# Opening of a fused decoder layer: five weight blocks per strip in place of three, two of them through saved partial sums

## The chip, the cores and the metric

The kernel runs on one NeuronCore of a Trainium2 chip. The metric is the device time of one execution in microseconds. Of the kernel before there are three timed executions, with a median of 1898.13 us, and one more that was profiled.

## The reference, cut to what matters

One decoder layer on 256 tokens of width 2048, all in f32: a SwiGLU feed-forward, a token mixer, a second SwiGLU, each between norms that are modulated by nine vectors computed from `c`.

```python
D_MODEL, SEQ, D_FF, N_MOD = 2048, 256, 5504, 9

def swiglu(h, w_in, w_out):
    gate, up = jnp.split(h @ w_in, 2, axis=-1)
    return (jax.nn.silu(gate) * up) @ w_out

def sandwich(x, fn, g_pre, g_post, shift, scale, gate, res_w):
    h = rms_norm(x, g_pre) * (1.0 + scale[:, None]) + shift[:, None]
    y = rms_norm(fn(h), g_post)
    return x + res_w * gate[:, None] * y

def reference(...):
    cond = jax.nn.silu(c)
    mod = cond @ ada_w[l] + ada_b[l]                 # ada_w: 2048 x 18432
    sh1, sc1, gt1, sh2, sc2, gt2, sh3, sc3, gt3 = jnp.split(mod, N_MOD, axis=-1)
    x = sandwich(x, swiglu with ffn1_w_in, ffn1_w_out, norm_g[0], norm_g[1], sh1, sc1, gt1, 0.5)
    x = sandwich(x, token_mixer ...,                   norm_g[2], norm_g[3], sh2, sc2, gt2, 1.0)
    x = sandwich(x, swiglu with ffn2_w_in, ffn2_w_out, norm_g[4], norm_g[5], sh3, sc3, gt3, 0.5)
    return x
```

The change touches the start: the two vectors `sh1` and `sc1`, the modulated `h` of the first feed-forward, and the first column blocks of `h @ ffn1_w_in`.

## The kernel before

**Products in two parts.** Every weight is split on the chip into a rounded part and a rest: ScalarE copies `w_raw` to `w_hi` (L781 in the opening, L601 later), VectorE subtracts to get `w_lo` (L1286, L983). `xT` is split the same way. TensorE then makes three products for each chunk of 128 rows: hi by hi, lo by hi, hi by lo (L1557 to L1559, or L1790, L1791, L1796 where the parts of `xT` come late). A **unit** is two chunks for both tiles of 128 tokens, so 12 matmuls of 512 columns. A **block** is 512 columns of the feed-forward's input matrix over all 16 chunks: 8 units. Its result fills one of the four PSUM pairs `ps_g`, `ps_u`, `ps_t`, `ps_y` (two banks each, 128 x 512 for each tile of tokens). Eight units make a group; the first feed-forward has 33 groups (264 units), each with 4 loads of 1 MB on SyncE's queue. The ring of `w_hi` and `w_lo` has 4 places: ScalarE may write the one of unit v when unit v-4 has been used (`pe_used`), and `w_raw` has four slots of two units.

**The modulation vectors.** `cond @ ada_w` is no matmul here. VectorE multiplies each piece of `ada_w` by its 128 values of `cond` and adds it to an accumulator (L1270, L1273; later L1015, L1017 on whole rows of 2048), and TensorE sums over the partitions at the end. Vectors 0 and 1 (`sh1`, `sc1`) are needed before the first product. They are made in **strips** of columns, `STRIP_CHUNKS = ((0, 4), (4, 4), (8, 4), (12, 2), (14, 2))`: the columns of a strip are the rows of `xT` that the units of this strip need. A tile is 1 MB of `ada_w` (two loads, one for each vector), a strip of 4 chunks has 8 tiles, one of 2 chunks has 4. The tiles go round in four slots, and SyncE issues a tile when the one four before it has been used.

**The opening.** For each strip TensorE does the units of this strip for three blocks (`OPENING = 3`: the gate block 0 in `ps_g`, the up block 0 in `ps_u`, the gate block 1 in `ps_t`). All three stay in PSUM until the last strip, and `ps_y` serves the column sums. A strip of 4 chunks has 6 units, one of 2 chunks has 3. Ahead of the last unit of a strip TensorE runs filler matmuls (`warm`, L1655: 24, 24, 0, 0 calls), then `first_sums` of the next strip (L1780, L1781: 16 calls of one column, 8 for a short strip), then the last unit. VectorE makes the new columns of `modcol` (L1294 to L1296), ScalarE scales `xT_raw` and rounds it (L695, L698), VectorE makes the rest (L1302), and the next strip's units may start. The order of all this is written out by hand for each engine, as is the order of loads on SyncE's queue.

**After the opening.** Block 0 has both halves, so `h = silu(gate) * up` (L796, `h_mul` L1039), a transpose of `h` on TensorE (`transpose_h`, L1621, 8 calls) into `ps_t`, and its products with the output matrix (`out_group`). The groups then follow as in-gate, in-up, out for each block (`hidden`). Blocks that `on_vector` names are transposed by VectorE (`turn_hidden`, L1062) instead. From unit 24 on the six other modulation vectors of this layer's first half are made beside it: 96 tiles (`ada_raw`, 1 MB each, issued by GpSimd, L541), tile a after unit `24 + 12 * a // 5`. The accumulators of four of them are transposed and summed at blocks `ROWS_AT` (`turned_half` on TensorE, `column_sums` on VectorE, L1073).

## Time and profile before

| what | value |
|---|---|
| median of the three timed executions | 1898.13 us (1897.89 to 1899.44) |
| profiled execution, its own time | 1899.21 us |
| its span | 1897.4 us |
| TensorE busy in the span | 1854.0 us, 98% |
| VectorE busy | 1495.9 us, 79% |
| ScalarE busy | 856.9 us, 45% |
| moved by DMA | 486.84 MB, mean 257 GB/s |

The profiled time is 1.81 us above its span, and 1.08 us above the median. Busy time of TensorE counts every matmul, the filler calls too. In the page's picture of 40 slices (47.4 us each), TensorE is at nine tenths or more in all but the first, and the DMA engines are at nine tenths or more in the first fourteen and fall to five to seven tenths after that.

### The profile page before, as it was taken

What the parts mean: (1) busy time and instruction counts of PE and PEld (TensorE: products, weight loads), DVE (VectorE), ACT (ScalarE), POOL (GpSimd) and SP (SyncE); (2) the same over time, 40 slices, a digit from 0 to 9 for tenths busy, and PEclk for the clock granted to TensorE, in tenths of its full rate; (3) what the DMA queues carried; (4) which work ended last, traced back from release to release, by engine and by line L of the source; (5) the groups of instructions that cost most, each with busy time, mean ns of one, the idle gap of its engine ahead of it and who ended that gap; (6) DMA issues with size and microseconds to landing.
All of it is one profiled execution on the core that took longest, in us unless ns stands there. A gap on an engine that the chain in (4) does not pass through costs nothing.

```text
span 1897.4 us, 21957 instructions
## 1 busy us (share of the span) xinstructions
PE 1854.0 (98%) x8743; PEld 1545.2 (81%) x8743; DVE 1495.9 (79%) x1633; ACT 856.9 (45%) x1095; POOL 82.0 (4%) x151
## 2 busy tenths in 40 slices
PE   6999999999999999999999999999999999999997
PEld 6878888888888889877778887888888888888895
DVE  5989989999989989975876587677777785676576
ACT  4244443443443444574666446544444434443443
POOL 0001000000000000010000010000000000000000
PEclk9999999999999999999999999999999999999998
DMA  9999999999998999655444454666776655556552
GB/s 369 369 372 360 341 363 332 353 342 346 356 347 316 389 342 343 246 161 181 149 134 134 162 176 167 231 233 237 250 249 234 240 191 198 189 198 213 175 199 78
DMA packets 208677, 486.84 MB, mean 257 GB/s; under 512 B 8560, under 2 KB 29760, under 8 KB 193472
## 3 DMA queue, kind: packets, MB, share of 16 engines
q1 hardware_dynamic: 191648, 365.72, 55.9%
q0 software_dynamic: 16224, 117.47, 16.5%
q10 hardware_dynamic: 704, 2.25, 0.3%
q8 instruction: 69, 1.13, 0.2%
q14 instruction: 32, 0.26, 0.0%
HBM read 483.31 MB, written 2.10 MB: 256 GB/s over the span
## 4 chain that ended last, share of the span: by engine, by line
PE 83%; DVE 10%; DMA 2%; issue 2%; ACT 1%; SPq 1%; ACTq 0%; DVEq 0%; POOL 0%
PE ps_u L1557 10%; PE ps_u L1559 10%; PE ps_u L1558 10%; PE ps_g L1557 8%; PE ps_g L1559 8%; PE ps_g L1558 8%; PE ps_y L1558 4%; PE ps_y L1559 4%; PE ps_y L1557 4%; PE ps_t L1557 4%; PE ps_t L1559 4%; PE ps_t L1558 4%; DVE w_lo L983 3%; DVE arena L1017 2%; DVE arena L1273 1%
## 5 line engine op out<-in xcount | busy, mean ns | idle before, releaser
L601 ACT ACTIVATE w_hi<-w_raw 128x1024 fp32r<-128x1024 f32 (+2 forms) x604 | 628.5, 1042 | 873.3 <-PE ps_u L1559 303.7
L983 DVE TENSOR_TENSOR w_lo<-w_raw,w_hi 128x1024 fp32r<-128x1024 f32 (+2 forms) x604 | 717.8, 1198 | 313.2 <-ACT w_hi L601 310.9
L1557 PE MATMUL ps_u<-w_hi,xT_hi 128*128 128x512 f32 (+2 forms) x880 | 342.6, 389 | 3.7 <-DVE w_lo L1286 1.4
L1559 PE MATMUL ps_u<-w_hi,xT_lo 128*128 128x512 f32 (+2 forms) x880 | 338.5, 385 | 0.0
L1558 PE MATMUL ps_u<-w_lo,xT_hi 128*128 128x512 f32 (+2 forms) x880 | 338.4, 385 | 0.0
L1557 PE MATMUL ps_g<-w_hi,xT_hi 128*128 128x512 f32 (+1 forms) x816 | 319.0, 391 | 0.7 <-DVE w_lo L983 0.4
L1559 PE MATMUL ps_g<-w_hi,xT_lo 128*128 128x512 f32 (+1 forms) x816 | 314.5, 385 | 0.0
L1558 PE MATMUL ps_g<-w_lo,xT_hi 128*128 128x512 f32 (+1 forms) x816 | 314.2, 385 | 0.0
L1017 DVE SCALAR_TENSOR_TENSOR arena<-ada_raw,cond,arena 128x2048 f32<-128x2048 f32 x108 | 253.3, 2345 | 5.8 <-DMA ada_raw<-in_ada_w 5.7
L1557 PEld LDWEIGHTS ps_u<-w_hi,xT_hi 128*128 128x128 f32 x880 | 165.2, 188 | 37.3 <-issue 3.1
L1559 PEld LDWEIGHTS ps_u<-w_hi,xT_lo 128*128 128x128 f32 x880 | 165.2, 188 | 31.8
L1558 PEld LDWEIGHTS ps_u<-w_lo,xT_hi 128*128 128x128 f32 x880 | 165.3, 188 | 30.3
L1557 PEld LDWEIGHTS ps_g<-w_hi,xT_hi 128*128 128x128 f32 x816 | 153.2, 188 | 34.3 <-DVE w_lo L983 4.0
L1559 PEld LDWEIGHTS ps_g<-w_hi,xT_lo 128*128 128x128 f32 x816 | 153.1, 188 | 29.9
L1558 PEld LDWEIGHTS ps_g<-w_lo,xT_hi 128*128 128x128 f32 x816 | 153.3, 188 | 28.4
L1557 PE MATMUL ps_y<-w_hi,hT_hi 128*128 128x512 f32 x320 | 124.7, 390 | 0.0
L1559 PE MATMUL ps_y<-w_hi,hT_lo 128*128 128x512 f32 x320 | 124.5, 389 | 0.0
L1558 PE MATMUL ps_y<-w_lo,hT_hi 128*128 128x512 f32 x320 | 124.5, 389 | 0.0
L1559 PE MATMUL ps_t<-w_hi,hT_lo 128*128 128x512 f32 x320 | 124.5, 389 | 0.0
L1557 PE MATMUL ps_t<-w_hi,hT_hi 128*128 128x512 f32 x320 | 124.5, 389 | 0.0
L1558 PE MATMUL ps_t<-w_lo,hT_hi 128*128 128x512 f32 x320 | 124.5, 389 | 0.0
L541 POOL DMA_DIRECT2D ada_raw<-in_ada_w x112 | 60.5, 540 | 992.8 <-DVE arena L1017 861.8
(323 smaller groups left out, 1900.0 us busy)
## 6 DMA issues: line engine op xcount, KB each, us to landing
w_raw<-in_ffn_w_in SPq DMA_DIRECT2D x157, 1024.0 KB, 6.2
ada_raw<-in_ada_w POOLq DMA_DIRECT2D x112, 1024.0 KB, 7.1
w_raw<-in_ffn_w_out SPq DMA_DIRECT2D x80, 1024.0 KB, 6.7
w_raw<-in_mix_w_in SPq DMA_DIRECT2D x32, 1024.0 KB, 5.1
ada_raw<-in_ada_w SPq DMA_DIRECT2D x32, 512.0 KB, 9.1
arena<-in_ada_w SPq DMA_DIRECT2D x32, 512.0 KB, 9.6
w_raw<-in_mix_w_out SPq DMA_DIRECT2D x16, 1024.0 KB, 5.0
w_raw<-in_ffn_w_in SPq DMA_DIRECT2D x16, 768.0 KB, 6.1
```

The costliest lines, as they stand in the source:

```text
L541: pool.dma_start(ada_raw[:, a % 2, :], ada_v[k, :, mod * D:(mod + 1) * D]).then_inc(ada_later[a % 2], 16)
L601: nc.scalar.activation(w_hi[:, u % 4, 0:n, 0:width], w_raw[:, s, 2 * hf:2 * hf + n, 0:width], ACT.Copy).then_inc(hi_done, 3 if g in EARLY_ ...
L983: nc.vector.tensor_tensor(w_lo[:, u % 4, 0:n, 0:width], w_raw[:, s, 2 * hf:2 * hf + n, 0:width], w_hi[:, u % 4, 0:n, 0:width].bitcast(F32) ...
L1017: ins = nc.vector.scalar_tensor_tensor(acc[:, pos, :], ada_raw[:, a % 2, :], cond[:, k:k + 1], acc[:, pos, :], ALU.mult, ALU.add)
L1273: ins = nc.vector.scalar_tensor_tensor(part, raw, weight, part, ALU.mult, ALU.add)
L1557: nc.tensor.matmul(o, a_hi[:, k, rows], w_hi[:, b, c, 0:width], start=start, stop=False)
L1558: nc.tensor.matmul(o, a_hi[:, k, rows], w_lo[:, b, c, 0:width], start=False, stop=False)
L1559: ins = nc.tensor.matmul(o, a_lo[:, k, rows], w_hi[:, b, c, 0:width], start=False, stop=stop)
```

## The change

- `OPENING = 5`: each strip now has units for five blocks, gate and up of blocks 0 and 1 and the gate of block 2. There are four strips of 4 chunks, with 10 units each, so 40 units in place of 24.
- There are only four PSUM pairs. Three blocks stay (`ps_g`, `ps_u`, `ps_t`). Blocks 3 and 4 of the table (up 1 and gate 2) share `ps_y` in turn. After a strip's two units of such a block, ScalarE copies `ps_y` to `partial` in SBUF (`save_partial`), and in the next strip TensorE puts it back with an identity matmul of 512 columns in f32 for each tile (`take_partial`). The order in a strip is kept, resident, kept, resident, resident (`block_of`); in the last strip the resident ones come first, and the last block ends in `ps_g`.
- `first_products`: both products of the first tile of strips 1, 2 and 3 are made by ScalarE.
- `first_sums` reads its two addends from `even` and `odd`, both of one strip's width; the filler ahead of it is 6 calls each time. On SyncE's queue a strip's five loads of weights alternate with the first four tiles of the next strip, and the other four tiles follow; each of these 13 loads is 1 MB, where a full strip had 11.
- The six later vectors start at unit 40, one tile every 11/5 units. `start_acc` of vectors 2 and 5 moves into the row of loads. `on_vector` leaves out block 1, and `ROWS_AT` is (4, 5, 7, 9).

```diff
@@ -41,7 +41,7 @@
-ROWS_AT = (3, 5, 7, 9)
+ROWS_AT = (4, 5, 7, 9)
@@ -56,19 +56,20 @@
-STRIP_CHUNKS = ((0, 4), (4, 4), (8, 4), (12, 2), (14, 2))
+STRIP_CHUNKS = ((0, 4), (4, 4), (8, 4), (12, 4))
 STRIPS = len(STRIP_CHUNKS)
-FULL = sum(n == 4 for _, n in STRIP_CHUNKS)
-OPENING = 3
+OPENING = 5
+KEPT = 3
+BLOCK_COLS = (0, DFF, NB, DFF + NB, 2 * NB)
+STRIP_UNITS = 2 * OPENING
 STRIP_TILES = [2 * n for _, n in STRIP_CHUNKS]
 ADA_PRE = sum(STRIP_TILES)
...
+MODS_LATER = ((3, 1), (4, 3), (6, 2), (7, 3), (2, 1), (5, 0), (8, 3))
 SUMMED = (3, 4, 6, 7)
...
+UNIT_FFN1 = [11 * a // 5 for a in range(6 * KD)]
 UNIT_FFN2 = [16 + 8 * a for a in range(KD)]
 
...
+def block_of(s, i):
+    return (3, 0, 4, 1, 2)[i] if s < STRIPS - 1 else i
...
-    return i < FBLOCKS - 1 and (f == 1 or i in (1, 3, 5, 7))
+    return i < FBLOCKS - 1 and (f == 1 or i in (3, 5, 7))
...
                 load_ada(a)
+                if a == 2 * KD + 4:
+                    pool.wait_ge(turned_done, 2)
+                    start_acc(2, 1)
+                if a == 3 * KD:
+                    start_acc(5, 0)
...
+            def save_partial(s, e):
+                act.wait_ge(pe_used, STRIP_UNITS * s + 4 * e + 2)
+                nc.scalar.activation(partial[:, e, :, :], ps_y[:, :, :], ACT.Copy).then_inc(partial_saved, 1)
+            def first_products(s):
+                act.wait_ge(ada_landed[0], 32 * ((first_count(s, 0) - 1) // 4) + 32)
+                act.wait_ge(ada_done, first_count(s, 0) - 1)
+                need(act, cols_done, s - 1)
+                raw = first_slots[0].rearrange("p (m k n) -> p m k n", m=2, k=2)
+                for k in range(2):
+                    ins = nc.scalar.activation((even, odd)[k][:, s % 2, :, :], raw[:, :, k, :], ACT.Copy, scale=cond[:, k:k + 1])
+                ins.then_inc(ada_done, 1)
             for s in range(STRIPS):
+                start = STRIP_UNITS * s
                 first_hi(start)
+                first_hi(start + 1)
+                first_xt_hi(2 * s)
+                first_hi(start + 2)
+                first_xt_hi(2 * s + 1)
+                if s + 1 < STRIPS:
+                    first_products(s + 1)
+                for i in range(3, 6):
                     first_hi(start + i)
+                if s < STRIPS - 1:
+                    save_partial(s, 0)
+                    for i in range(6, STRIP_UNITS):
+                        first_hi(start + i)
+                    save_partial(s, 1)
+            act.wait_ge(pe_used, 8 * OPENING - 8)
...
+                start, more = STRIP_UNITS * s, s + 1 < STRIPS
                 first_lo(start)
                 first_lo(start + 1)
                 first_columns(s)
+                if more:
+                    sums_at[0] = sums_at[1] = (ada_done, first_count(s + 1, 0))
+                first_xt_lo(2 * s)
+                first_lo(start + 2)
+                first_xt_lo(2 * s + 1)
+                if more:
                     first_ada(s + 1, 1)
+                first_lo(start + 3)
+                first_lo(start + 4)
+                if not more:
+                    for i in range(5, 8):
+                        first_lo(start + i)
+                    h_mul(0, 0, NB, start + 4)()
+                    first_lo(start + 8)
+                    first_lo(start + 9)
+                    continue
+                first_ada(s + 1, 2)
+                first_lo(start + 5)
+                first_lo(start + 6)
+                first_ada(s + 1, 3)
+                first_lo(start + 7)
+                first_lo(start + 8)
+                first_ada(s + 1, 4)
+                first_lo(start + 9)
+                for i in range(5, STRIP_TILES[s + 1]):
+                    first_ada(s + 1, i)
...
+            def take_partial(e, ps):
+                for t in range(TILES):
+                    nc.tensor.matmul(ps[:, t, :], ident[:, :], partial[:, e, t, :], start=True, stop=False)
             warm(12, ps_g)
             first_sums(0)
             for s in range(STRIPS):
+                last = s == STRIPS - 1
+                if s:
+                    pe.wait_ge(modcol_done, s + 1)
+                if s and not last:
+                    take_partial(0, ps_y)
+                for i in range(STRIP_UNITS):
+                    v, (q, hf) = STRIP_UNITS * s + i, divmod(i, 2)
+                    b, pair = block_of(s, q), 2 * s + hf
+                    ps = (ps_g, ps_u, ps_t, ps_y, ps_g if last else ps_y)[b]
+                    if last and b == KEPT and hf == 0:
+                        take_partial(0, ps_y)
+                    if b == KEPT + 1 and hf == 0:
+                        if last:
+                            pe.wait_ge(silu_done, 2)
+                            transpose_h(0, 4, 0)
+                        else:
+                            pe.wait_ge(partial_saved, 2 * s + 1)
+                        if s:
+                            take_partial(1, ps)
+                    if i == STRIP_UNITS - 1 and not last:
+                        pe.wait_ge(partial_saved, 2 * s + 2)
+                        warm(6, ps_y)
                         first_sums(s + 1)
                     pe.wait_ge(lo_done, v + 1)
+                    if q == 0:
```

VectorE at the turn from the first strip to the second. `w_lo` is the split of a unit, L1273 and L1270 (L1283 in the changed kernel) the products of a tile of `ada_w`, two calls for each tile, L1294 (L1304) the start of the new columns. Before, from the `w_lo` of the first strip's last unit to the new columns:

```order
L1286 TENSOR_TENSOR w_lo<-w_raw,w_hi 128x1024
L1273 SCALAR_TENSOR_TENSOR arena<-arena,cond 128x2x512
L1273 SCALAR_TENSOR_TENSOR arena<-arena,cond 128x1024
L1273 SCALAR_TENSOR_TENSOR arena<-arena,cond 128x2x512
L1273 SCALAR_TENSOR_TENSOR arena<-arena,cond 128x1024
L1270 TENSOR_SCALAR arena<-ada_raw,cond 128x2x512
L1270 TENSOR_SCALAR arena<-ada_raw,cond 128x1024
L1286 TENSOR_TENSOR w_lo<-w_raw,w_hi 128x1024 x2
L1294 TENSOR_TENSOR bias<-ps_y,bias 128x2x4
```

In the changed kernel, from the `w_lo` of its units 7 and 8 to the same point:

```order
L1296 TENSOR_TENSOR w_lo<-w_raw,w_hi 128x1024 x2
L1283 SCALAR_TENSOR_TENSOR arena<-ada_raw,cond,arena 128x1024 x2
L1296 TENSOR_TENSOR w_lo<-w_raw,w_hi 128x1024
L1283 SCALAR_TENSOR_TENSOR arena<-ada_raw,cond,arena 128x1024 x2
L1283 SCALAR_TENSOR_TENSOR arena<-arena,cond 128x1024 x4
L1296 TENSOR_TENSOR w_lo<-w_raw,w_hi 128x1024 x2
L1304 TENSOR_TENSOR bias<-ps_y,bias 128x2x4
```

What moved: ahead of the sums three whole tiles of `ada_w` now stand behind the last `w_lo` of the strip where two did, and the first tile of the strip after (L1270) is gone from VectorE. A strip has 10 `w_lo` where it had 6, and 7 tiles on VectorE where it had 8.

TensorE at the same turn, from the filler to the first unit of the second strip, before:

```order
L1655 MATMUL ps_y<-ident 128x128 x24
L1780 MATMUL ps_y<-ones,arena 128x1
L1781 MATMUL ps_y<-ones,arena 128x1
...
L1781 MATMUL ps_y<-ones,arena 128x1
L1557 MATMUL ps_t<-w_hi,xT_hi 128x512
L1558 MATMUL ps_t<-w_lo,xT_hi 128x512
...
L1559 MATMUL ps_t<-w_hi,xT_lo 128x512
L1790 MATMUL ps_g<-w_hi,xT_hi 128x512
L1791 MATMUL ps_g<-w_lo,xT_hi 128x512
```

In the changed kernel, from its filler to the first unit of the second strip:

```order
L1657 MATMUL ps_y<-ident 128x128 x6
L1781 MATMUL ps_y<-ones,arena 128x1
L1782 MATMUL ps_y<-ones,arena 128x1
...
L1782 MATMUL ps_y<-ones,arena 128x1
L1559 MATMUL ps_t<-w_hi,xT_hi 128x512
L1560 MATMUL ps_t<-w_lo,xT_hi 128x512
...
L1561 MATMUL ps_t<-w_hi,xT_lo 128x512
L1803 MATMUL ps_y<-arena,ident 128x512 x2
L1791 MATMUL ps_y<-w_hi,xT_hi 128x512
L1792 MATMUL ps_y<-w_lo,xT_hi 128x512
```

What moved: 6 filler calls stand where 24 stood, and a restored partial sum (L1803) stands ahead of the first unit, which now goes to `ps_y`.

## Rows read from the trace of the kernel before

**Rows 1.** Windows of the opening; columns: busy us of each engine, TensorE clock, DMA share, GB/s
```profile
44.60:192.26 147.66, 143.15 (x704) 120.31 (x705) 132.80 (x137) 56.37 (x65) 10.53 (x14) 0.95 1.03 368
44.60:49.80 5.20, 5.20 (x12) 4.08 (x13) 5.20 (x6) 3.34 (x5) 0.00 (x0) 0.50 1.05 387
67.10:97.17 30.07, 28.77 (x153) 24.94 (x153) 26.75 (x28) 9.58 (x12) 0.00 (x0) 0.89 1.06 384
70.30:77.20 6.90, 6.90 (x20) 5.56 (x20) 5.05 (x8) 5.03 (x8) 0.00 (x0) 0.51 1.05 387
101.00:104.50 3.50, 3.50 (x10) 2.69 (x10) 2.12 (x5) 1.65 (x4) 0.00 (x0) 0.51 1.05 385
```

**Rows 2.** TensorE in time: start, us, place (first unit, a unit, unit 24, unit 40)
```profile
44.58 0.77 PE L1790 MATMUL ps_g<-w_hi,xT_hi 128*128 128x512 f32 x1 [2.40 <-ACT xT_hi L698]
...
52.58 0.39 PE L1557 MATMUL ps_u<-w_hi,xT_hi 128*128 128x512 f32 x1
...
53.26 0.39 PE L1557 MATMUL ps_u<-w_hi,xT_hi 128*128 128x512 f32 x1
...
147.71 0.50 PE L1557 MATMUL ps_u<-w_hi,xT_hi 128*128 128x512 f32 x1 [0.89 <-DVE arena L1039]
...
192.26 0.39 PE L1557 MATMUL ps_g<-w_hi,xT_hi 128*128 128x512 f32 x1
```

**Rows 3.** TensorE in time: filler, first and last sums of strips 1 and 2
```profile
60.74 5.52 PE L1655 MATMUL ps_y<-ident 128*128 128x128 f32 x48
67.10 0.38 PE L1780 MATMUL ps_y<-ones,arena 128*128 128x1 f32 x2 [0.84 <-DVE arena L1273]
...
70.63 0.56 PE L1781 MATMUL ps_y<-ones,arena 128*128 128x1 f32 x2
...
97.17 0.38 PE L1780 MATMUL ps_y<-ones,arena 128*128 128x1 f32 x2 [1.30 <-DVE arena L1273]
...
100.54 0.36 PE L1781 MATMUL ps_y<-ones,arena 128*128 128x1 f32 x2
```

**Rows 4.** Waits of TensorE from 44 to 192 us
```profile
PE ps_y L1780 <- DVE arena L1273: 2.1, 2, 1.3
PE ps_u L1557 <- DVE w_lo L1286: 1.4, 1, 1.4
```

**Rows 5.** VectorE in time, end of strip 1's tiles to the next strip's first
```profile
62.18 4.87 DVE L1273 SCALAR_TENSOR_TENSOR arena<-arena,cond 128x1024 f32<-128x1024 f32 x4
...
69.01 2.36 DVE L1286 TENSOR_TENSOR w_lo<-w_raw,w_hi 128x1024 fp32r<-128x1024 f32 x2 [0.64 <-ACT w_hi L781]
71.29 0.16 DVE L1294 TENSOR_TENSOR bias<-ps_y,bias 128x8 f32<-128x8 f32 x1
...
73.53 0.69 DVE L1302 TENSOR_TENSOR xT_lo<-arena,xT_hi 128x512 fp32r<-128x512 f32 x1 [1.82 <-ACT xT_hi L698]
```

**Rows 6.** TensorE in time: two f32 matmuls of 256 columns, start to start, and 8 transposes
```profile
156.01 1.04 PE L1621 MATMUL ps_t<-ident,arena 128*128 128x128 f32 x8
...
1031.86 0.59 PE L1910 MATMUL ps_y<-ada_raw,arena 128*128 128x256 f32 x2
1032.29 0.59 PE L1901 MATMUL ps_y<-ada_raw 128*128 128x256 f32 x2
```

**Rows 7.** Windows of 24 units after the opening, columns as above
```profile
190.00:256.00 66.00, 65.95 (x290) 54.02 (x289) 63.69 (x58) 27.36 (x27) 5.52 (x11) 1.00 0.95 352
256.00:322.00 66.00, 66.00 (x305) 54.99 (x304) 57.69 (x42) 27.00 (x26) 4.77 (x9) 1.00 0.94 342
```

**Rows 8.** VectorE's later tiles, and the loads of these tiles
```profile
L1017 DVE SCALAR_TENSOR_TENSOR arena<-ada_raw,cond,arena x85: 2335/2345/2353, 195.0 to 768.6; 128x2048 f32<-128x2048 f32 x85
...
  DMA ada_raw<-in_ada_w: 2.9, 2
...
L541 POOL DMA_DIRECT2D ada_raw<-in_ada_w x75: 530/530/530, 205.9 to 699.5; - x75
...
DMA to landing us min/median/max: 5.1/7.2/9.7
```

194 lines of the change are left out of this document (62 added, 132 removed).

## The prediction

> **What bounds the kernel now.** I began with the page's busy shares and its 40 slices: TensorE is full everywhere but at the start. So I took the opening in windows, then the waits, then the engines in order of time. From the first unit at 44.58 us to unit 40, the point where the changed opening ends, there are 147.7 us [rows 2]. Beyond unit 40 TensorE has no gap worth naming [rows 7], and the work behind it hardly changes. The question is therefore one number: how long the changed kernel takes from its first unit to its unit 40.
>
> A unit takes 2.72 us: three matmuls go out every 0.68 us at the full clock [rows 2]. The 40 units are 108.8 us of the 147.7. The other 38.9 us are what the change can get at. They split up as follows.
>
> - Column sums: 3.7 us for each of the strips 1 and 2 (67.10 to 70.8, 97.17 to 100.8) [rows 3], half of that for each of the two short strips: 11.1 us.
> - Filler: 48 matmuls in 5.5 us [rows 3], with the step to what follows 5.6, twice, and a half of it (12 calls) once: 14.0 us.
> - Real waits: 2.1 + 1.4 us, and 0.9 ahead of unit 24, 4.4 us [rows 2, 4].
> - Eight transposes: 1.04 us as shown [rows 6], 0.9 from start to the next start.
> - Half clock. The granted clock is 0.51 for the 6.9 us from 70.3 and for the 3.5 us from 101.0, that is 1.2 GHz in place of 2.4 [rows 1]. In the first, sums still run for some 0.7 us of it, the rest is units at half speed, 3.1 us lost. The second loses 1.7. From 44.6 to 49.8 us, with the first unit, it is 0.50 [rows 1]: 2.6. Together 7.4 us.
>
> These are 37.8 us. 1.1 us stay unexplained, and I carry them over unchanged.
>
> The two other resources are nearly full at the same time. In the 30.07 us from sums to sums VectorE is busy 26.75 us and the DMA engines move 384 GB/s [rows 1]. A strip has 11 loads of 1.049 MB, 11.5 MB, which at 384 GB/s is 30.0 us. The strip of before is as long as its transfers. That makes the idea plausible: TensorE has filler and waits in a stretch set by DMA, and a strip's two units of a further block, which cost one more load, can fill it.
>
> **The strip of the changed kernel, from three sides.**
>
> - *DMA*: 13 loads, 13.6 MB, at 384 GB/s 35.5 us.
> - *VectorE*: a `w_lo` takes 1.14 us from one to the next (a pair 2.36), a tile of `ada_w` 2.39 (four calls 4.87, two calls a tile), an `xT_lo` 0.6, the columns 0.45 (71.29 to 71.72) [rows 5]. Ten, seven, two and one of them: 11.4 + 16.7 + 1.2 + 0.45 = 29.8 us. Then what it must wait for. The sums take 3.7 us plus 0.5 until it sees them, covered by two `w_lo` only (2.3): 1.9. ScalarE scales and rounds the new `xT`: 1.8 [rows 5]. The second `xT` pair and the `w_hi` that follow in ScalarE's row have no row of their own; 0 to 3 us, I take 1.5, nearer the second wait of 0.64 that stands in [rows 5], counted twice. Sum 35.0 us.
> - *TensorE*: 10 units 27.2, sums 3.7, six filler calls 0.7, two restored partial sums 1.7. Sum 33.3 us, so it waits 1.7 us for VectorE's last tile ahead of the sums. Before, it waited 0.84 and 1.30 there, behind a long filler [rows 3].
>
> The three are within 2.2 us of each other: no engine has anything left to give inside the strip.
>
> **Restored partial sums.** Two f32 matmuls of 256 columns stand 0.43 us apart from the next pair [rows 6], so one takes 0.215 and one of 512 columns 0.43 us. `take_partial` has two, 0.86 us, and there are six: 5.2 us. The trace has none of 512 columns; the bound below is 0.23 (what a rounded one of that width takes [rows 2]), the bound above four times that, and I take the value from the f32 rows, which are nearest in kind. The Trainium skill (FP8 and Floating Point Precision, TensorE Precision Notes) says that true FP32 makes 4 passes through the array. By that rule a restored sum would be 1.7 us and the six 5.1 us more than I count; the row of the 256-column f32 matmuls speaks for two passes, not four.
>
> **ScalarE.** It gains six copies of `ps_y` and six products, about 1 us each. It is busy 9.58 us of a strip of 30.07 [rows 1], so these 4 us a strip are hidden. If they were not, `w_hi` would be late and VectorE with it; that is inside the 0 to 3 us above.
>
> **The clock.** Here is the term that decides. Before each of the two strips where the clock fell, TensorE had been through its wait and the one-column sums: 0.84 + 3.7 = 4.5 us and 1.30 + 3.7 = 5.0 us with almost no columns streamed [rows 3]. It fell at the end of both, although 5.5 us of filler stood ahead. In the changed kernel this stretch is 1.7 + 3.7 = 5.4 us, with 0.7 us of filler ahead and full sums at all three turns. So I expect the clock to fall three times. The two falls cost 3.1 and 1.7 us; the next ones begin earlier, so that part of the sums is slow too. I take 3.0 us each, 9.0; bounds 0 (no fall) and 5.
>
> **The sum from the first unit to unit 40:** units 108.8, sums 3 x 3.7 = 11.1, filler 2.1, restored sums 5.2, transposes 0.9, waits 3 x 1.7 = 5.1, half clock 2.6 + 9.0 = 11.6, unexplained 1.1. In all 145.9 us, against 147.7: **1.8 us less.** The first unit itself starts where it did: the tiles of strip 0, the sums and the first columns are untouched. What went: 11.9 us of filler. What came: restored sums, longer waits, more half clock.
>
> **Behind unit 40.** Block 1 is now transposed by TensorE: 0.9 us more [rows 6]. VectorE is relieved of that turn, but its later tiles come every 2.2 units instead of every 2.4. In 24 units that is 0.9 tiles of 2.34 us [rows 8], 2.1 us more on top of 63.7 of 66 us in a stretch with turned blocks, or 57.7 without [rows 7]. Block 4 also gets the column sums, some 2.5 us. So one stretch is over-full by 2 us. VectorE works ahead: it may be up to three units in front, less the 2.3 us of the two splits, so about 5.9 us. This covers it, and I count 0. If the cover is gone the price is those 2 us.
>
> DMA there: 24 units need 24 loads of half a MB and 10.9 tiles, 24.0 MB in 65.3 us, 368 GB/s against 342 to 352 now [rows 7], and 384 seen in the opening. A tile must be there 9.7 us after its slot is free (two steps of 5.98 less 2.34); now it lands after 7.2 us, at most 9.7 [rows 8], plus 0.5 for the issue. Nearly always in time; counted 0. The two `start_acc` on GpSimd fall between two loads and delay one by less than a step; 0 as well.
>
> **Forecast:** 1.8 less and 0.9 more, 0.9 us less in all. The profiled execution of 1899.21 us would be 1898.3. It lies 1.1 us above the median of the timed ones, so I give 1898.13 - 0.9, rounded to 1897.2 us. About 0.2%, 3.8 us, is what a measurement of this kernel can tell from no change. The forecast is thus "same", because one wait was traded for another.
>
> **Rivals.**
>
> 1. *The clock holds.* If ten dense units keep it up through the sums, the 9.0 us are gone: 1888.2 us. For it: in the short strips before, sums of half the length did not bring it down. Against: both full-length sums did. Chance 0.25.
> 2. *The tiles behind unit 40 come late (slower).* The place is VectorE's row in the first feed-forward. If 368 GB/s is more than that mix of queues gives, each tile lands after its slot's 9.7 us, `w_lo` stands behind the waiting tile, and TensorE waits for `w_lo`. It decides from a median landing of about 9.2 us (with 0.5 for the issue). VectorE has next to no spare time in the turned blocks to catch up; 0.1 us for each of some 90 tiles is 9 us: 1906 us. For it: 0.95 of the DMA engines' time is used at 352 GB/s [rows 7]. Against: 1.06 at 384 [rows 1]. Chance 0.16.
> 3. *Restored sums take four passes.* 5.1 us more, less up to 2 us where they only eat the wait ahead of the sums: 1900 to 1902 us. Chance 0.12.
> 4. *The change as forecast,* 1892 to 1901 us. Chance 0.47.
>
> The range takes in cases 3 and 4, most of 1 and the cheaper half of 2: 1888 to 1904 us. Faster by over 0.2%: 0.25 from case 1 and 0.11 from the lower end of case 4 (the falls of the clock cheaper by 1 us each), 0.36. Slower: case 2 whole, 0.04 of case 3 and 0.04 of case 4, 0.24. Same: 0.40.
>
> **What the profile of the changed kernel should show.** Sums about every 38 us; a wait of TensorE for a tile of 1 to 3 us ahead of each; restored sums with 0.43 us between them; a granted clock of 0.5 behind each of the sums of strips 1, 2 and 3; unit 40 between 189 and 192 us; no waits for `w_lo` worth over 2 us behind it. The forecast is wrong if unit 40 comes before 187 us, if the clock stays at 1, or if TensorE has gaps between 200 and 700 us.

## The result, and the profile of the changed kernel

| | before | changed |
|---|---|---|
| median of the timed executions | 1898.41 us (1897.54 to 1899.65, 8 runs) | 1903.92 us (1902.25 to 1905.93, 8 runs) |
| ratio to before, 95% interval | | 1.003 [1.0019, 1.0041] |
| span of the profiled execution | 1897.4 us | 1901.7 us |

The changed kernel is slower: 5.5 us by the medians, 4.3 us by the two spans. Forecast was 0.9 us less, "same". The kernel moved the other way. The measured value is just inside the range, whose upper end is 1904, and it lies there by luck: the range reached that far to take in half of rival 2, whose mechanism is not what happened.

The page of the changed kernel, busy time of the engines and the granted clock in 40 slices:

```profile
PE 1858.7 (98%) x8691; PEld 1543.9 (81%) x8691; DVE 1482.8 (78%) x1592; ACT 869.7 (46%) x1107; POOL 81.7 (4%) x151
PEclk9999999999999999999999999999999999999999
```

Neither says where the time is; the windows do, with the columns of [rows 1]. The first is from the first unit to unit 40, the second one period from sums to sums, the next three the stretches at half clock, and the last two the windows of [rows 7]:

```profile
44.60:194.04 149.44, 146.56 (x644) 118.29 (x645) 110.22 (x105) 68.54 (x77) 1.76 (x3) 0.92 0.90 326
74.20:114.30 40.10, 39.11 (x172) 31.30 (x172) 30.37 (x30) 17.64 (x20) 0.00 (x0) 0.91 0.96 341
77.70:84.50 6.80, 6.80 (x17) 5.11 (x18) 3.01 (x6) 5.62 (x9) 0.00 (x0) 0.52 1.05 385
118.70:122.10 3.40, 3.40 (x10) 2.60 (x10) 1.52 (x2) 3.37 (x6) 0.00 (x0) 0.54 1.06 388
156.30:163.10 6.80, 6.80 (x19) 5.45 (x20) 3.01 (x6) 5.09 (x8) 0.25 (x1) 0.52 0.99 393
190.00:256.00 66.00, 66.00 (x297) 54.73 (x296) 60.40 (x43) 27.29 (x26) 5.30 (x10) 1.00 0.94 346
256.00:322.00 66.00, 66.00 (x297) 54.75 (x296) 58.27 (x42) 27.14 (x27) 5.83 (x11) 1.00 0.98 362
```

The opening took 149.4 us where 147.7 were before [rows 1] and 145.9 were forecast. The period is 40.1 us and not 38, and in it VectorE is busy 30.4 us and the DMA engines move 341 GB/s, less than the 384 of before: neither of them sets it now, TensorE does. The clock fell at all three turns, as forecast.

How much of this is the pair of executions that were traced? The opening of the kernel before stands in three more traces (the two controls and the run with its tiles at 2.2 units, below): 149.4, 147.5 and 149.5 us from first unit to unit 40, with the clock at 0.5 in other stretches. That of the changed kernel stands in two more (tiles earlier, no block turned): 149.3 and 149.5. So the 1.8 us between the two openings is near the upper end of what such pairs show; by the means it is 0.9. The table of terms further down doesn't hang on this, since it is made within one trace.

TensorE in time at the first turn (the end of a strip's tenth unit, filler, sums, half clock), and from the transposes of the last strip over the restored sum to unit 40:

```profile
71.55 0.39 PE L1561 MATMUL ps_t<-w_hi,xT_lo 128*128 128x512 f32 x1
71.78 1.50 PE L1657 MATMUL ps_y<-ident 128*128 128x128 f32 x12
74.24 0.38 PE L1781 MATMUL ps_y<-ones,arena 128*128 128x1 f32 x2 [0.96 <-DVE arena L1283]
...
77.75 0.56 PE L1782 MATMUL ps_y<-ones,arena 128*128 128x1 f32 x2
78.17 0.77 PE L1559 MATMUL ps_t<-w_hi,xT_hi 128*128 128x512 f32 x1
...
185.96 1.03 PE L1623 MATMUL ps_t<-ident,arena 128*128 128x128 f32 x8
186.83 1.88 PE L1803 MATMUL ps_g<-arena,ident 128*128 128x512 f32 x4
188.15 0.79 PE L1559 MATMUL ps_g<-w_hi,xT_hi 128*128 128x512 f32 x1
188.78 0.40 PE L1560 MATMUL ps_g<-w_lo,xT_hi 128*128 128x512 f32 x1
...
194.04 0.39 PE L1559 MATMUL ps_y<-w_hi,hT_hi 128*128 128x512 f32 x1
```

Two things are to be seen here. The six filler calls stand as `x12`, and the two calls of a restored sum as `x4`: a matmul call with f32 operands leaves **two** records. (The transposes don't: eight calls stand as `x8`.) And a restored sum takes from 186.83 until the second matmul behind it goes out at 188.78, 1.95 us, where an ordinary step is 0.23. It costs 1.72 us, twice the 0.86 that were counted.

Waits of TensorE from 44 to 760 us (columns: us in total, times, longest), to be held against [rows 4]:

```profile
PE ps_y L1781 <- DVE arena L1283: 2.9, 3, 1.0
PE ps_y L1791 <- ACT xT_hi L684: 2.4, 1, 2.4
PE ps_u L1559 <- DVE w_lo L992: 0.9, 2, 0.4
PE ps_g L1559 <- DVE w_lo L992: 0.8, 3, 0.5
```

The last two lines lie behind unit 40. They are small, but they are where the other part of the loss shows. Two of these waits, with the row of VectorE that leads to them:

```profile
478.89 0.50 PE L1559 MATMUL ps_g<-w_hi,xT_hi 128*128 128x512 f32 x1 [0.15 <-DVE w_lo L992]
...
485.46 0.47 PE L1559 MATMUL ps_u<-w_hi,xT_hi 128*128 128x512 f32 x1 [0.44 <-DVE w_lo L992]
```

```profile
475.82 1.78 DVE L1071 STREAM_TRANSPOSE spare<-arena 32x256 f32<-32x256 f32 x4
477.61 1.23 DVE L992 TENSOR_TENSOR w_lo<-w_raw,w_hi 128x1024 fp32r<-128x1024 f32 x1
478.87 1.79 DVE L1071 STREAM_TRANSPOSE spare<-arena 32x256 f32<-32x256 f32 x4
480.69 1.23 DVE L992 TENSOR_TENSOR w_lo<-w_raw,w_hi 128x1024 fp32r<-128x1024 f32 x1
481.83 2.35 DVE L1026 SCALAR_TENSOR_TENSOR arena<-ada_raw,cond,arena 128x2048 f32<-128x2048 f32 x1
484.10 2.35 DVE L992 TENSOR_TENSOR w_lo<-w_raw,w_hi 128x1024 fp32r<-128x1024 f32 x2
```

A window over this stretch, with the columns of [rows 1]:

```profile
465.00:485.00 20.00, 19.77 (x85) 15.40 (x83) 19.67 (x25) 7.43 (x7) 3.65 (x5) 1.00 0.83 295
```

VectorE has no gap, and is busy 19.67 of the 20 us. It turns a block (four times four STREAM_TRANSPOSEs, 1.8 us a time) between its splits and tiles, and TensorE starts on these two `w_lo` as soon as they are made. Comparing where the same output tile begins in both traces gives the shift of the changed kernel against the kernel before:

| place (start before, us) | shift, us |
|---|---|
| unit 40 (192.26) | +1.8 |
| 348.49 | +2.2 |
| 481.72 | +3.7 |
| 615.56 | +4.7 |
| 683.42 | +4.8 |
| 803.37 and all that follows | +4.3 |

So 1.8 us of the 4.3 came in the opening and 2.5 behind it, 1.5 and 0.9 of them in the two stretches between 416 and 482 us and between 549 and 616 us, in each of which VectorE turns a block. The shifts are more than the waits of the list, 1.7 us: a record of TensorE lasts 0.39 us where the next is 0.23 behind it, so 0.16 us of each wait is hidden under the record ahead, and shorter delays don't show at all.

### The profile page after: what moved, and what is told of

The parts are those of the page before. It is cut to its first block, busy times and chain, and to the rows that moved or that the text cites. A ratio compares the mean times of both kernels' runs of the same rounds, so it can differ in the third digit from the quotient of the medians.

```text
span 1901.7 us, 21837 instructions
## 1 busy us (share of the span) xinstructions
PE 1858.7 (98%) x8691; PEld 1543.9 (81%) x8691; DVE 1482.8 (78%) x1592; ACT 869.7 (46%) x1107; POOL 81.7 (4%) x151
## 4 chain that ended last, share of the span: by engine, by line
PE 66%; DVE 6%; issue 1%; ACT 0%; DMA 0%; DVEq 0%; POOL 0%; ACTq 0%
PE ps_u L1559 8%; PE ps_u L1561 8%; PE ps_u L1560 8%; PE ps_g L1559 7%; PE ps_g L1561 7%; PE ps_g L1560 7%; PE ps_t L1559 3%; PE ps_t L1561 3%; PE ps_t L1560 3%; PE ps_y L1561 3%; PE ps_y L1560 3%; PE ps_y L1559 3%; DVE w_lo L992 2%; DVE arena L1026 1%; DVE arena L1039 1%
## 5 line engine op out<-in xcount | busy, mean ns | idle before, releaser
L591 ACT ACTIVATE w_hi<-w_raw 128x1024 fp32r<-128x1024 f32 (+2 forms) x588 | 612.2, 1042 | 862.3 <-PE ps_u L1561 296.0
L992 DVE TENSOR_TENSOR w_lo<-w_raw,w_hi 128x1024 fp32r<-128x1024 f32 (+2 forms) x588 | 699.5, 1199 | 303.6 <-ACT w_hi L591 301.5
L1559 PE MATMUL ps_u<-w_hi,xT_hi 128*128 128x512 f32 (+2 forms) x848 | 330.1, 389 | 1.8 <-DVE w_lo L992 1.0
L1561 PE MATMUL ps_u<-w_hi,xT_lo 128*128 128x512 f32 (+2 forms) x848 | 326.1, 385 | 0.0
L1560 PE MATMUL ps_u<-w_lo,xT_hi 128*128 128x512 f32 (+2 forms) x848 | 325.9, 384 | 0.0
L1559 PEld LDWEIGHTS ps_u<-w_hi,xT_hi 128*128 128x128 f32 x848 | 159.2, 188 | 34.4 <-issue 4.8
L1561 PEld LDWEIGHTS ps_u<-w_hi,xT_lo 128*128 128x128 f32 x848 | 159.1, 188 | 30.4
L1560 PEld LDWEIGHTS ps_u<-w_lo,xT_hi 128*128 128x128 f32 x848 | 159.3, 188 | 29.1
```

Of the source, the lines that this page charges most:

```text
L591: nc.scalar.activation(w_hi[:, u % 4, 0:n, 0:width], w_raw[:, s, 2 * hf:2 * hf + n, 0:width], ACT.Copy).then_inc(hi_done, 3 if g in EARLY_ ...
L992: nc.vector.tensor_tensor(w_lo[:, u % 4, 0:n, 0:width], w_raw[:, s, 2 * hf:2 * hf + n, 0:width], w_hi[:, u % 4, 0:n, 0:width].bitcast(F32) ...
L1559: nc.tensor.matmul(o, a_hi[:, k, rows], w_hi[:, b, c, 0:width], start=start, stop=False)
L1560: nc.tensor.matmul(o, a_hi[:, k, rows], w_lo[:, b, c, 0:width], start=False, stop=False)
L1561: ins = nc.tensor.matmul(o, a_lo[:, k, rows], w_hi[:, b, c, 0:width], start=False, stop=stop)
```

## Experiments

All ratios are to the kernel before, timed on the same chip in the same batch. "Less than the changed kernel" is worked out from the ratios: (ratio - 1.003) x 1899 us. It carries the intervals of two ratios, about 2.7 us up or down with eleven runs and 3.2 with five, and each trace is one execution. Where it matters, the mean granted clock of a kernel's runs is given: 0.001 of it is 1.9 us. It is 0.9905 over the eight runs of the changed kernel. Every trace also has 8 to 11 us at half clock at its very end, which no edit touches, so I take a difference of less than 0.0005 between two means as none.

### The opening

**Halved column sums.** The changed kernel sums 8 tiles of columns twice each, from `even` and from `odd`. Here VectorE adds the two first, and 14 filler calls stand in place of 6.

```diff
+            def add_halves(s):
+                dve.wait_ge(*sums_at[0])
+                dve.wait_ge(*sums_at[1])
+                nc.vector.tensor_tensor(even[:, s % 2, :, :], even[:, s % 2, :, :], odd[:, s % 2, :, :], ALU.add).then_inc(sums_whole, 1)
...
-                        nc.tensor.matmul(col, even[:, s % 2, m, c * P:(c + 1) * P], ones[:, 0:1], start=True, stop=False)
-                        ins = nc.tensor.matmul(col, odd[:, s % 2, m, c * P:(c + 1) * P], ones[:, 0:1], start=False, stop=True)
+                        ins = nc.tensor.matmul(col, even[:, s % 2, m, c * P:(c + 1) * P], ones[:, 0:1], start=True, stop=True)
...
-                        warm(6, ps_y)
+                        warm(14, ps_y)
```

> VectorE adds the two accumulators of a strip (1.2 us), the column sums are 8 calls in place of 16, and the filler ahead is 14 calls in place of 6. Theory D (the clock falls because TensorE streams almost no columns for the 0.96 us wait and the 3.7 us of sums): with sums of 1.8 us behind 3.2 us of filler the clock stays up at the turns to strips 1, 2 and 3, which gives back 2 to 3 us each, and the sums give 0.6 us each: unit 40 at 184 to 187, time 1894 to 1897. If the clock falls all the same: 1 to 2 us gained or none, since VectorE's row is 1.3 us longer in each strip: 1902 to 1904.

Measured 1896.52 us, ratio 0.9987 [0.9979, 0.9996]: 8.2 us less than the changed kernel, and faster than the kernel before. The first turn (filler, sums), then windows over the two places where the clock is low and over the stretch behind the third sums:

```profile
69.67 3.29 PE L1665 MATMUL ps_y<-ident 128*128 128x128 f32 x28
73.46 1.95 PE L1789 MATMUL ps_y<-ones,arena 128*128 128x1 f32 x16 [0.50 <-DVE arena L1296]
```

```profile
76.90:80.30 3.40, 3.40 (x11) 2.52 (x10) 1.92 (x2) 3.34 (x6) 0.00 (x0) 0.71 1.05 383
114.50:117.90 3.40, 3.40 (x12) 2.66 (x11) 1.62 (x2) 3.37 (x6) 0.00 (x0) 0.72 1.05 387
150.00:160.00 10.00, 10.00 (x52) 8.49 (x52) 7.03 (x10) 6.35 (x10) 1.23 (x2) 1.00 0.74 277
```

Behind the third sums the clock stays up; theory D's time came true, though the clock still fell at two of the three turns. From the first unit (42.36 us) to unit 40 (185.81) this trace has 143.45 us, 6.0 less than the changed kernel's 149.47. From the filler's start to the sums it is 3.79 us (69.67 to 73.46) where it was 2.46, since the addition lies on the path, and the sums are about 1.8 us shorter: the three turns save 1.4 us. The stretches at half clock went from 6.8 + 3.4 + 6.8 us to 3.4 + 3.4, which is 5.1 us of time. The stretch at half clock around the first unit costs 0.1 us more. 1.4 + 5.1 - 0.1 = 6.4, of which the trace shows 6.0. Another 2.2 us stand ahead of the first unit, where the first strip's sums are halved too; the first units of kernels with full sums lie between 42.4 and 44.9 us, so this part is uncertain. Within the opening the gain is the clock's more than the sums' own, and all runs bear it out: their mean granted clock is 0.9935, against 0.9905.

Which fall goes is not fixed. Three later runs have the same halved sums and 14 filler calls. With rounded copies the trace has two falls of 6.8 us, at the first and the third turn; with the last sums on VectorE two of 3.4 us, at the same two turns; with everything together three, of 6.8, 3.4 and 3.4 us.

**The same with 6 filler calls** (`warm(6, ps_y)`).

> The halved column sums alone, with 6 filler calls ahead of them as the changed kernel has, not 14: tells whether the shorter sums or the longer filler took away the third fall of the clock. Eight calls fewer are 1.9 us a turn; the wait for VectorE's last tile, 0.5 us behind 14 calls, becomes 1.5 to 2.4 us, so filler for wait leaves the time between units as it was. Theory A (the halved sums do it): the clock behaves as with 14 calls, two falls of 3.4 us, and the total is within 1.5 us of that run, 1895 to 1898 us. Theory B (the filler does it, and an idle wait in its place is as bad as the sums): three falls again, two of them 6.8 us long as in the changed kernel, 3 to 5 us more, 1899 to 1902 us.

Measured 1898.48 us, ratio 0.9999 [0.999, 1.0008]: 2.3 us more than with 14 calls, between the two theories by the time. The first turn:

```profile
69.48 1.50 PE L1665 MATMUL ps_y<-ident 128*128 128x128 f32 x12
73.27 1.95 PE L1789 MATMUL ps_y<-ones,arena 128*128 128x1 f32 x16 [2.29 <-DVE arena L1296]
```

From filler to sums it is 3.79 us again: eight calls fewer became 1.8 us more of waiting, nothing else moved. But the clock now falls three times, 3.4, 3.4 and 6.8 us. The half clock behind the third sums is 3.4 us of time, the opening in this trace is 3.1 us longer (42.17 to 188.74), and the timed runs differ by 2.3. The two intervals touch (0.9979 to 0.9996 and 0.999 to 1.0008), but the clock of all runs says the same: a mean of 0.9923 in these eleven against 0.9935 with 14 calls, which is 2.3 us. So filler in place of an idle wait of the same length is worth some 2 us here: it costs nothing where TensorE would wait anyway, and less of the run is at half clock.

**24 filler calls** in the changed kernel, with its full sums.

> The changed kernel with 24 filler calls ahead of each of the three sums where it has 6, the number that the kernel before has there. A call costs 0.25 us by the changed kernel's trace (six of them 1.50 us as 12 matmuls), so 18 more are 4.2 us at each turn, less the wait of 0.96 us that they cover: 3.3 us a turn, 9.8 us in all. Theory A (the clock falls because of the sums themselves; filler ahead of them does not matter): three falls as long as now, unit 40 about 10 us later, 1912 to 1915 us. Theory B (longer filler keeps the clock up in the sums, the fall then comes later or is shorter as in the kernel before, 3.5 us at half clock at the one turn): 1.5 to 5 us of the 9.8 come back, 1908 to 1912 us.

Measured 1909.99 us, ratio 1.0053 [1.0041, 1.0066]: 4.4 us more than the changed kernel by the ratios, 6.1 by the medians, inside theory B's range. At the first turn:

```profile
70.99 5.52 PE L1657 MATMUL ps_y<-ident 128*128 128x128 f32 x48
```

From the filler's start to the sums it is 5.36 us (70.99 to 76.35) where it was 2.46, 2.9 more at each turn, 8.7 together. The falls are 6.8, 3.4 and 3.4 us: the third one is half as long, 1.7 us back. The stretch at half clock at the first unit ends earlier too, worth 1.1 us, but it lies ahead of any filler, so that is no merit of it. 8.7 - 1.7 - 1.1 = 5.9; the trace has 5.8 (44.78 to 200.02). Filler beyond the wait it covers costs more than the clock gives back, and ahead of full sums it doesn't prevent the fall.

**Last partial sums added by VectorE.** Four restored sums in place of six; the last strip begins fresh sums, and VectorE adds `partial` to the finished ones.

```diff
-                    if last and b == KEPT and hf == 0:
-                        take_partial(0, ps_y)
...
-                        if s:
+                        if s and not last:
                             take_partial(1, ps)
...
+                        nc.vector.tensor_tensor(partial[:, e, :, :], ps[:, :, :], partial[:, e, :, :], ALU.add).then_inc(partial_added, 1)
```

> The last strip restores neither partial sum on TensorE; VectorE, which has gaps there, adds them afterwards (two additions of about 1.2 us). Theory A (each restored sum costs 1.7 us of TensorE's row, since one f32 call is two passes of 512 columns at each record, and the last strip has no other bound): unit 40 about 3.4 us earlier than the changed kernel's 194.0, so 190.6, and the time 3.4 us below the changed kernel's 1903.9: 1900.5. Rival B (the opening is set by transfers or by VectorE, TensorE's row has slack): unit 40 stays at 194 and the time at 1904.

Measured 1900.69 us, ratio 1.0007 [0.9999, 1.0016]: 4.4 us less than the changed kernel. Two restored sums at 1.72 us are 3.4 us, at the 0.86 of the prediction they would be 1.7; the timed runs, good to 2.7 us, can't tell these two apart, but they exclude rival B, no gain. Its trace has 2.0 us less from first unit to unit 40 (44.81 to 192.29): 3.4 less for the two sums, 0.7 more wait ahead of the sums, 1.7 more because the clock stayed down 3.4 us longer behind the first sums, 1.1 less at the first unit. Single traces of this opening scatter by such a stretch of half clock; the medians of the kernel before in its five batches lie within 1.0 us.

**All six restored from rounded copies**, with a rounded identity. This rounds the partial sums of two blocks.

```diff
-                nc.scalar.activation(partial[:, e, :, :], ps_y[:, :, :], ACT.Copy).then_inc(partial_saved, 1)
+                nc.scalar.activation(partial[e][:, :, :], ps_y[:, :, :], ACT.Copy).then_inc(partial_saved, 1)
...
-                    nc.tensor.matmul(ps[:, t, :], ident[:, :], partial[:, e, t, :], start=True, stop=False)
+                    nc.tensor.matmul(ps[:, t, :], ident_r[:, :], partial[e][:, t, :], start=True, stop=False)
```

> Partial sums are saved and restored in the rounded type, one pass in place of more (this rounds what the kernel computes). Theory A: a restored sum falls from 1.7 to 0.46 us. The two of the last strip give 2.5 us in full; the four in strips 1 and 2 give their 2.5 us a strip only as far as VectorE's last tile is not already awaited (wait of 0.96 us before each of the sums), so 1 to 3 us of the 5: 4 to 5.5 us in all, 1898.5 to 1900. If restored sums of 1.7 us are the whole loss and nothing else waits: 7.5 us, 1896.4. Rival B: no change, 1904.

Measured 1897.67 us, ratio 0.9994 [0.9985, 1.0003]: 6.8 us less than the changed kernel. One restored sum in its trace:

```profile
91.60 0.63 PE L1808 MATMUL ps_y<-hT_lo,ident_r 128*128 128x512 f32 x2
92.07 0.39 PE L1564 MATMUL ps_y<-w_hi,xT_hi 128*128 128x512 f32 x1
```

Two calls leave two records and take 0.47 us. That is 1.25 less than the 1.72 of the true f32 form, 7.5 us for six; and from first unit to unit 40 the trace (42.44 to 184.44) has 142.0 us, 7.5 less, with the clock down as long as in the changed kernel (17 us over the three turns). Theory A had expected up to half of the gain in the middle strips to turn into waits; the waits stayed at 0.96 us. This settles the price of a restored sum.

**First products back on VectorE**: `first_products` left out, the first tile of strips 1 to 3 in `first_ada` as the others.

```diff
-                if s + 1 < STRIPS:
-                    first_products(s + 1)
...
                 if more:
+                    first_ada(s + 1, 0)
                     first_ada(s + 1, 1)
```

> The changed kernel without one of its parts: the first product of each later strip is made by VectorE again and not by ScalarE. VectorE has one call of a tile more in each of the three later strips, 1.2 us, plus what it has to wait. If VectorE is what sets the length of a strip (TensorE waits 0.96 us for its last tile at each turn), each turn comes 1.2 us later, 3.6 us in all: 1906 to 1909 us, and the waits ahead of the sums grow to about 2.2 us. Rival (VectorE has slack that the trace of one run hides, transfers set the strip): within 1 us of the changed kernel, 1903 to 1905 us, the waits as they are.

Measured 1903.33 us, ratio 1.0021 [1.0012, 1.003]: no slower than the changed kernel, 1.7 us less by the ratios, 0.6 by the medians, with intervals that overlap. The rival came true as to the time and the waits: the one ahead of the sums is the same 0.96 us. That transfers set the strip, which it also says, doesn't fit the 341 GB/s of the period. VectorE of the changed kernel in the second strip shows why:

```profile
98.66 1.22 DVE L1296 TENSOR_TENSOR w_lo<-w_raw,w_hi 128x1024 fp32r<-128x1024 f32 x1
102.32 1.23 DVE L1296 TENSOR_TENSOR w_lo<-w_raw,w_hi 128x1024 fp32r<-128x1024 f32 x1 [2.44 <-ACT w_hi L765]
```

VectorE stands idle for 2.44 us for a `w_hi`, which in turn needs a slot that TensorE frees: it has caught up. With the first tile back on VectorE that wait is still there:

```profile
99.32 1.23 DVE L1294 TENSOR_TENSOR w_lo<-w_raw,w_hi 128x1024 fp32r<-128x1024 f32 x1 [2.44 <-ACT w_hi L765]
```

The two calls of the tile, 1.3 us together from one start to the next, took the place of shorter waits ahead of it (in the changed kernel 1.46 us for ScalarE's products, 0.71 and 0.69 for a `w_hi`). What TensorE waits for ahead of the sums is thus not VectorE's load over the strip. My reading, which no run tested by itself, is the order of its row at the end: the last `w_lo` follows TensorE's pace, and three tiles, 7.2 us, stand behind it.

**Two cuts at once.** The halved sums with the last partial sums added by VectorE, and the halved sums with rounded copies:

> The changed kernel with two of its terms cut at once: VectorE adds the even and odd half of the column sums into one tile, so that TensorE makes half as many one-column matmuls (14 filler calls in place of 6 ahead of them), and in the last strip VectorE adds the saved partial sums to the finished ones, so that TensorE restores four of the six partial sums and not six. Each part alone gave a ratio to the kernel before of 0.9987 and 1.0007, against 1.003 of the changed kernel: 8.2 and 4.4 us less. Theory A, the terms are independent (the half clock behind the sums depends on the sums alone, the restored sums on their number): 12 us less than the changed kernel, 1891 to 1894 us, unit 40 near 182 to 185 us in the trace. Theory B, both gains came out of the same wait (VectorE's last tile ahead of the sums, which grows as soon as TensorE is faster): only the larger of the two stays, 1895 to 1897 us, and TensorE waits 2 us or more for a tile ahead of each of the sums.

> The halved column sums as in the run beside this, and all six partial sums restored from rounded (fp32r) copies with a rounded identity. It rounds the partial sums of two blocks, which the kernel before does not. If a restored sum of rounded type takes a quarter of the time of a true f32 one (0.23 us for 512 columns against 0.86), the two calls cost 0.46 and not 1.7 us, six of them 7.5 us less. Theory A (independent terms): 7 to 8 us less than the halved sums alone, 1888 to 1890 us. Theory B (the strip is as long as VectorE and the transfers make it, so TensorE's saved 2.5 us in each middle strip turn into a wait ahead of the sums): two thirds of it are lost, 1893 to 1896 us, with 2 us or more of wait ahead of each of the sums and more half clock behind them.

Measured 1893.79 us, ratio 0.9965 [0.9953, 0.9978], and 1890.13 us, ratio 0.9947 [0.9933, 0.9961]: 12.3 and 15.8 us less than the changed kernel, the sums of the single gains being 12.6 and 15.0. By the times the terms are independent, as theory A has it in both; theory B's 1895 to 1897 and 1893 to 1896 us are missed. From first unit to unit 40 it takes 139.7 and 140.1 us. The trace of the second is less clean than its times: the wait ahead of the sums grew from 0.5 to 1.3 and 1.9 us at the first and third turn, with the clock down for 6.8 us behind each, which is what theory B foresaw. Something of it is there, then, and it doesn't decide the time. The first of the two leaves nothing out and rounds nothing that the kernel before doesn't, and beats both kernels by 0.35% and 0.65%; the second gives away some precision for 0.2% more, with intervals that overlap.

### Behind unit 40

**Tiles made earlier.** A first try against the lateness: three of the later tiles in the opening, the others every 7/3 units.

```diff
-UNIT_FFN1 = [11 * a // 5 for a in range(6 * KD)]
+UNIT_FFN1 = [7 * a // 3 for a in range(6 * KD)]
...
-        ada_at = [8 * (G_FFN[0] + OPENING) + u for u in UNIT_FFN1]
+        ada_at = [34, 36, 38] + [8 * (G_FFN[0] + OPENING) + u for u in UNIT_FFN1[:-3]]
...
+                if v in ada_at:
+                    ada_unit(ada_at.index(v))
```

> The later vectors' first three tiles move into the last strip of the opening, behind units 34, 36 and 38, where VectorE waits 1.4 us or more for each w_hi, and the others come every 7/3 units in place of 11/5. Theory C (VectorE is over-full in the stretches with turned blocks 5 and 7 and makes TensorE wait, 1.5 us in each behind unit 40): these waits fall to 0.6 or less in all, 2 to 2.5 us gained, 1901.5. Against it: if the waits come from where tiles and turns meet and not from their number, less than 1 us. A tile in the last strip should not move unit 40 by more than 0.5 us.

Measured 1905.7 us, ratio 1.0035 [1.0023, 1.0048]: not better than the changed kernel. The opening is as long, and the trace is 1.9 us behind that of the changed kernel by 808 us. Up to 760 us it has 3.1 us of waits for `w_lo` in three places where the changed kernel has 1.7 in five, and it is 0.7 us behind there. The larger part of the 1.9, 1.6 us, comes between 772 and 789 us, where the last tiles now fall and TensorE waits 1.06 us for a `w_lo`. A slightly wider spacing alone is no cure; where the tiles fall against the turned blocks moved too, and which of the two did it was not separated.

**No block turned by VectorE** in the first feed-forward of the changed kernel.

```diff
-    return i < FBLOCKS - 1 and (f == 1 or i in (3, 5, 7))
+    return i < FBLOCKS - 1 and f == 1
```

> The changed kernel, but VectorE no longer turns (transposes) any block of the first feed-forward: TensorE transposes all of them, 0.9 us more for each of three blocks, 2.6 us. Theory C (the 2.5 us that the changed kernel loses behind unit 40 are VectorE's w_lo coming late in the stretches in which it also turns a block, since the tiles of ada_w now come every 2.2 units and not every 2.4): the waits of TensorE for w_lo and the slow units near 480 and 615 us are gone, the shift against the kernel before between unit 40 and 700 us is only the 2.6 us of transposes, and the total stays within 0.7 us of the changed kernel, 1903 to 1905 us. Theory D (the 2.5 us are late transfers or something else of the chip, not VectorE's share): the gaps stay where they are, and the total is 2.6 us more, 1906 to 1907 us.

Measured 1901.4 us, ratio 1.0009 [1.0, 1.0018]: 4.0 us less than the changed kernel, although TensorE has three times eight transposes more. No wait of TensorE for `w_lo` is left between 200 and 760 us. Between unit 40 and 803 us the shift against the changed kernel is 1.3 us less: the 2.6 us of transposes were paid, and 3.9 given back. The place and the waits are as theory C has them, and theory D, gaps that stay and 2.6 us more, is refuted. Theory C expected no net gain; the trace shows 1.3 us of one. The other 2.7 of the 4.0 us don't show in this trace. They are within what two ratios are good to. Some of it may be clock (a mean of 0.9912 in the eleven runs against 0.9905, 1.3 us), and in both traces that is low only up to 163 us, ahead of anything that the edit touches, and at the end.

Were the tiles late, as rival 2 of the prediction has it? In the trace of the changed kernel they land after a median of 7.4 us, at most 9.4, where that rival needed about 9.2. VectorE waited for one in five places, 6.6 us in all, but never between 231 and 508 us or between 509 and 637, where the losses of 1.5 and 0.9 us arose.

**The control: the same edit of the kernel before.** This was put on record for it first, ahead of a run that proved to be without the edit:

> The kernel before, with TensorE transposing the four blocks of the first feed-forward that VectorE turns: control for the same edit of the changed kernel, which made that one 4 us faster. Four times eight transposes are 3.7 us more for TensorE. Theory C (VectorE falls behind in the turned stretches only because the changed kernel has a tile of ada_w every 2.2 units; here it is every 2.4): VectorE has next to nothing to give back, 1 us at most, so 2.5 to 3.7 us slower, 1902 to 1903 us. Rival E (a block turned by VectorE costs TensorE as much as its own transposes in either kernel): 0 to 1 us, 1898.5 to 1900.5 us.

What ran was the kernel before, unchanged: 1898.97 us, ratio 1.0002 [0.9993, 1.001]. It says nothing on the theories, only how little two sets of runs of one kernel differ, and how much two traces do: the clock fell here for 6.8 and 6.8 us at the first two turns, not 6.8 and 3.4, and unit 40 starts 149.4 us behind the first unit (44.61 to 193.97), not 147.7. The control with the edit (`f == 1` in place of `f == 1 or i in (1, 3, 5, 7)`):

> The kernel before, with TensorE transposing the four blocks of the first feed-forward that VectorE turns (blocks 1, 3, 5 and 7). The run named x12_before_off was meant to be this, but its kernel was the kernel before unchanged. Four times eight transposes are 3.7 us more for TensorE. Theory C (VectorE falls behind in the turned stretches only because the changed kernel has a tile of ada_w every 2.2 units; here it is every 2.4): VectorE has next to nothing to give back, 0.6 us, so 3 to 3.7 us slower, 1901.5 to 1903 us. Rival E (a block turned by VectorE costs TensorE as much as its own transposes in either kernel): 0 to 1 us, 1898.5 to 1900.5 us.

Measured 1901.5 us, ratio 1.0014 [1.0005, 1.0023]: 2.7 us slower. The sign is the opposite one, and nearer theory C than rival E. In the trace the shift against the kernel before grows by 1.9 us from unit 40 to 803 us, for transposes of 3.5: VectorE's turns cost TensorE 1.6 us even here, where rival E needed 2.5 or more, but clearly less than they save. In the kernel before it pays to let VectorE turn blocks, in the changed kernel it doesn't.

**The spacing of the tiles alone, in the kernel before.**

```diff
-UNIT_FFN1 = [12 * a // 5 for a in range(6 * KD)]
+UNIT_FFN1 = [11 * a // 5 for a in range(6 * KD)]
```

> The kernel before with one number changed: the later tiles of ada_w come every 2.2 units, as in the changed kernel, and not every 2.4. The opening is untouched. Theory C (the closer tiles are what makes VectorE late behind unit 40 in the changed kernel): the same 2 to 2.5 us appear here between the opening and 700 us, in the stretches in which VectorE turns a block, with waits of TensorE for w_lo; 1900.5 to 1902 us, a ratio of 1.001 to 1.0015. Rival F (they come from what the opening leaves behind, the order of the two resident blocks and the column sums moved to block 4): nothing here, 1898.5 to 1899.5 us, a ratio of 1.000, and no waits for w_lo in the trace beyond the one of 0.6 us.

Measured 1904.88 us, ratio 1.0036 [1.0024, 1.0049]: 6.8 us slower by the ratio, from one number. Its waits of TensorE from 190 to 760 us, the unit after the worst of them, and VectorE ahead of it:

```profile
PE ps_g L1557 <- DVE w_lo L983: 5.2, 4, 2.3
PE ps_u L1557 <- DVE w_lo L983: 0.5, 1, 0.5
```

```profile
484.60 0.39 PE L1559 MATMUL ps_g<-w_hi,xT_lo 128*128 128x512 f32 x1
487.31 0.50 PE L1557 MATMUL ps_g<-w_hi,xT_hi 128*128 128x512 f32 x1 [2.32 <-DVE w_lo L983]
```

```profile
480.68 1.23 DVE L983 TENSOR_TENSOR w_lo<-w_raw,w_hi 128x1024 fp32r<-128x1024 f32 x1
481.82 2.34 DVE L1017 SCALAR_TENSOR_TENSOR arena<-ada_raw,cond,arena 128x2048 f32<-128x2048 f32 x1
484.20 1.79 DVE L1062 STREAM_TRANSPOSE spare<-arena 32x256 f32<-32x256 f32 x4
486.02 2.36 DVE L983 TENSOR_TENSOR w_lo<-w_raw,w_hi 128x1024 fp32r<-128x1024 f32 x2
```

A tile and a turn, 4.2 us, stand between two splits, where TensorE uses up a unit every 2.72. The effect is larger than theory C said. The kernel before turns four blocks where the changed one turns three, and its block 1 costs 3.2 us in this trace (the shift grows from 2.1 to 5.3 between 192 and 215 us), but not by VectorE alone: in two places TensorE's wait (1.93 and 2.32 us) was followed by a stretch at half clock,

```profile
215.60:219.00 3.40, 3.40 (x8) 2.69 (x9) 3.40 (x3) 0.00 (x0) 0.00 (x0) 0.51 1.01 393
488.70:492.10 3.40, 3.40 (x10) 2.63 (x9) 3.40 (x3) 0.35 (x1) 0.02 (x1) 0.51 0.99 366
```

which costs 1.7 us more each time. This trace is of an execution of 1909.33 us, where the median of the five is 1904.88, and its mean clock is 0.990 where the other four have 0.991 or 0.992, so these falls are hardly in every run: behind unit 40 the trace loses 8.0 us, without the two falls 4.6. A wait of 1.89 us in the run with tiles made earlier (483.61 us) was followed by no fall. The spacing is shown to be enough to cause such a loss, without any change of the opening.

**Everything together**: halved sums, last partial sums on VectorE, no turned block.

> Three cuts together: halved column sums with 14 filler calls, the last partial sums added by VectorE, and no block of the first feed-forward turned by VectorE. The first two together measured 0.9965 of the kernel before, the third took the changed kernel from 1.003 to 1.0009. If they add up (the third acts behind unit 40, the first two ahead of it): 0.9944, 1888 to 1891 us. If the third one gains only because the opening leaves VectorE behind in its work, and the halved sums have cured that already, the transposes on TensorE cost their 2.6 us and give nothing back: 1894 to 1896 us.

Measured 1892.79 us, ratio 0.9965 [0.9954, 0.9977], the same as without the third cut. The gain of 4.0 us did not add up, nor were 2.6 us lost. Its trace, of an execution of 1895.04 us, shows where the third cut's gain went. Held against the trace with the first two cuts, the opening is 3.1 us longer from first unit to unit 40 (142.8 for 139.7) with the same instructions: the clock fell three times. From unit 40 to 737 us the third cut gives back 1.1 us, as it gave 0.9 in the changed kernel up to 749. Then two waits for `w_lo`, 0.70 and 1.35 us, stand at 750 and 756 us and lose 2.1 us again. Ahead of each VectorE had waited for a tile of `ada_w`:

```profile
741.61 2.35 DVE L1030 SCALAR_TENSOR_TENSOR arena<-ada_raw,cond,arena 128x2048 f32<-128x2048 f32 x1 [2.98 <-DMA ada_raw<-in_ada_w]
752.53 2.35 DVE L1030 SCALAR_TENSOR_TENSOR arena<-ada_raw,cond,arena 128x2048 f32<-128x2048 f32 x1 [1.70 <-DMA ada_raw<-in_ada_w]
```

So late transfers, the mechanism of the prediction's rival 2, do reach TensorE here, in the last and narrow block. In the changed kernel VectorE waits 2.13 us for a tile at 755.72 us and TensorE only 0.15 behind it. One trace doesn't tell whether every run has this loss.

## Why the prediction was wrong

From first unit to unit 40, by the terms of the prediction:

| term | predicted, us | in the trace, us |
|---|---|---|
| 40 units | 108.8 | 108.8 |
| three sums | 11.1 | 11.1 |
| filler | 2.1 | 4.5 (3 x 1.50) |
| six restored sums | 5.2 | 10.3 (6 x 1.72) |
| transposes | 0.9 | 0.9 |
| waits | 5.1 | 2.9 |
| half clock at the first unit | 2.6 | 2.8 |
| half clock at three turns | 9.0 | 8.5 (half of 6.8 + 3.4 + 6.8) |
| unexplained | 1.1 | -0.3 |
| sum | 145.9 | 149.5 |

- **The step that failed first** is the one that said "Two f32 matmuls of 256 columns stand 0.43 us apart from the next pair [rows 6], so one takes 0.215 and one of 512 columns 0.43 us". The `x2` of [rows 6] was one call of two records; 0.43 us was the price of one matmul of 256 columns, 0.86 that of one of 512, and `take_partial` costs 1.72. The filler was read in the same wrong way: 24 calls are the `x48` of [rows 3], 0.23 us each, so six are 1.4 us. The order of instructions, which counts calls, stood beside the rows and would have told it: 24 filler calls there, 48 matmuls in the trace. The prediction's own filler sum has it right for before, where it takes 12 calls as half of the 48 records and 2.8 us, and wrong for after, where six calls are 0.7. Together 7.5 us too little.
- **Rival 3 was the mechanism that came true**, restored sums at four passes' time. Its price of 5.1 us more was right; its 1900 to 1902 us were not, for want of the filler and of the loss behind unit 40. The prediction set it at 0.12, on the strength of the row it had misread. The Trainium skill (FP8 and Floating Point Precision, TensorE Precision Notes) says that true FP32 takes four passes; the trace agrees: 1.72 us against 0.47 of the rounded form, 3.7 times.
- **Its offset failed too.** The prediction let up to 2 us of it be eaten by the wait ahead of the sums. The wait is indeed 2.2 us less than forecast, but it did not shrink because the strip grew longer: it is 0.96 us at each turn, with the first products on VectorE as without them. The prediction took it as a difference of totals, 35.0 us for VectorE less 33.3 for TensorE, and the 33.3 leave out the 3.0 us of half clock that it added afterwards. With them no wait would have been left. The DMA and VectorE sums of 35.5 and 35.0 us a strip were no bounds for a period of 40.1.
- **The clock was forecast right** as to its falls: three of them, 8.5 us for 9.0. That the size agrees so well is in part luck: behind the same full sums, other traces lost 6.8 us (first products on VectorE) and 10.2 (last sums on VectorE). Halved sums give some of it back (mean clock 0.9905 to 0.9923), halved sums with the wait filled more (0.9935).
- **ScalarE's products** were costed at nothing, which holds, but they also bring nothing: VectorE had time to spare in the strip, one wait of 2.44 us and several shorter ones.
- **Behind unit 40** the second step failed: "This covers it, and I count 0". Forecast was 0.9 us, the trace has 2.5. The account was made over 24 units, with 5.9 us of cover. But the load is not even: in the eight units in which a block is turned, VectorE has splits, tiles and turns back to back, cover is used up within them, and TensorE waits. It is rival 2 by its place and sign. Its mechanism, late transfers, is not what happened in these stretches: the tiles land after 7.4 us in the median, VectorE waits for none of them there, and with no turned blocks and the same transfers the waits vanish.
- **Of the signs that it gave**, sums every 38 us (40.1) and unit 40 between 189 and 192 us (194.0) failed. The wait ahead of the sums is at the lower end of its 1 to 3 us, and the waits for `w_lo` behind unit 40 stayed under 2 us (1.7), so that sign did not tell of the loss there.
- The sum of both misses: 3.6 us in the opening and 1.6 behind it, 5.2, which is the 4.3 measured in the spans plus the 0.9 forecast. The medians differ by 5.5; the last 1.2 us are in no trace.

What stays open: how much of the 2.5 us is spacing and how much the place of the tiles against the turned blocks, since 2.2 against 2.4 units was only tested in the kernel before; why the clock falls for 3.4 us at one turn and 6.8 at another; and whether the late tiles that ate the gain of the third cut are in every run.

## What to carry to other kernels

Before a price is taken from a row with a count, hold that count against the number of calls in the program: a true f32 matmul leaves two records and takes almost four times what a rounded one takes, so where saved sums are restored through TensorE, round them or add them on VectorE. Test the cover of a prefetching engine over the few units in which its extra work bunches, not over the whole period. Fill a wait that TensorE has anyway, up to its length and no further: it is free, and here less of the run was at half clock. Before a difference of 2 us between two traces is explained, look at a second trace of the same kernel.

## What the runs showed of the hardware

- A true f32 matmul of 128 x 512 takes 0.86 us at the full clock and shows as two records; with both operands of rounded type it takes 0.23 us and shows as one. An f32 transpose of 128 x 128 on TensorE takes 0.11 us and shows as one record (eight of them 0.87 us).
- The same 3.79 us between the last matmul of a strip and the sums, once with 28 filler records and 0.50 us idle and once with 12 and 2.29 us idle, gave a mean granted clock of 0.9935 and of 0.9923 over eleven runs each, and 2.3 us between the timed ratios. In the two traces it was two falls of the clock and three.
- The same instructions don't always meet the same clock: behind the column sums for strips 1 and 2 of the kernel before it fell for 6.8 and 3.4 us in one trace, for 6.8 and 6.8 in another and for 3.4 and 6.8 in a third.
- Of three waits for `w_lo` amid full work, those of 1.93 and 2.32 us were followed by 3.4 us at half clock, which is 1.7 us on top of the wait; one of 1.89 us was not.
